# Eight gathers between the folds of the last gate, earlier routing steps on ScalarE, and rows spread evenly over the UP stage

## The reference, cut to what matters

```python
q = (h @ w_q).reshape(T, 8, 256)                       # T = 256 tokens, 8 heads
s1, s2 = q[..., :128] @ k1.T, q[..., 128:] @ k2.T      # 128 keys each
v1, i1 = top_k(s1, 16); v2, i2 = top_k(s2, 16)
top, pos = top_k(v1[..., None] + v2[..., None, :], 16) # 16 experts of 16384 a head
idx = take_along_axis(i1 * 128 + i2, pos)
act = gelu(einsum('thkd,td->thk', u_tab[idx], h)) * softmax(top)
ff = einsum('thk,thkd->td', act, v_tab[idx])
x = x + gt_f * rms_norm(ff, g_post_ffn)                # gt_f: the last gate, silu(c) @ w_ada + b_ada
```

## Time and profile before

| | us |
|---|---|
| median of 3 runs | 1793.8 |
| profiled execution | 1799.25 |
| its span | 1797.1 |
| TensorE busy | 1700.1 (95%) |
| VectorE busy | 1395.3 (78%) |
| ScalarE busy | 600.9 (33%) |
| GpSimd busy | 352.6 (20%) |
| moved by DMA | 646.75 MB, 360 GB/s |

### The profile page before, as it was taken

The page is one execution under the profiler, slowest core; times in us unless marked ns, Lnnn a source line. Parts: engine busy times, 40 slices in busy tenths (PEclk is TensorE's granted clock), DMA queues, the critical chain, the costliest instruction groups (busy, mean ns, idle before and its releaser), DMA issues.

```text
span 1797.1 us, 26702 instructions
## 1 busy us (share of the span) xinstructions
PE 1700.1 (95%) x9810; PEld 1475.6 (82%) x9810; DVE 1395.3 (78%) x2170; ACT 600.9 (33%) x1062; POOL 352.6 (20%) x266
## 2 busy tenths in 40 slices
PE   7999999999999899949999879999999999999998
PEld 6888888544999899949999879988778777777786
DVE  4668899967776497895876747169899998999997
ACT  3001222401543321013332103244444444544454
POOL 1000000011000121231122212014324333243310
PEclk9999999999999999979999999999999999999999
DMA  9998766799899999988999999799999999999995
GB/s 380 421 421 335 279 250 247 261 404 389 300 348 283 304 416 370 417 331 336 421 383 385 421 420 414 269 335 406 390 387 377 387 389 391 391 377 385 389 382 205
DMA packets 112121, 646.75 MB, mean 360 GB/s; under 512 B 16339, under 2 KB 16931, under 8 KB 50211
## 3 DMA queue, kind: packets, MB, share of 16 engines
q1 hardware_dynamic: 71570, 384.88, 55.2%
q0 software_dynamic: 34976, 252.75, 35.6%
q10 hardware_dynamic: 5488, 7.93, 1.6%
HBM read 639.08 MB, written 5.26 MB: 359 GB/s over the span
## 4 chain that ended last, share of the span: by engine, by line
PE 53%; DMA 25%; DVE 9%; issue 9%; ACT 2%; POOL 1%; DVEq 0%; ACTq 0%; SPq 0%; POOLq 0%
PE ps L1441 20%; PE ps L1082 14%; DMA raw<-in_peer_v 8%; DMA raw<-in_w_ada 7%; PE ps L1166 6%; PE ps L1336 4%; DMA third<-third 3%; DMA big<-in_u_rows,mid_info 3%; DVE raw L1500 2%; PE ps L1177 2%; DMA big<-in_u_rows,row_info 2%; PE ps L1282 2%; PE ps L1123 1%; DVE big L1860 1%; DVE w_low L1482 1%
## 5 line engine op out<-in xcount | busy, mean ns | idle before, releaser
L1082 PE MATMUL ps<-early,raw 128*128 128x144 f32 x3840 | 494.6, 290 | 25.4 <-DMA raw<-in_peer_u 24.7
L1082 PEld LDWEIGHTS ps<-early,raw 128*128 128x128 f32 x3840 | 485.1, 194 | 29.6 <-issue 14.8
L782 ACT ACTIVATE w_hi<-raw 128x1024 fp32r<-128x1024 f32 x204 | 214.7, 1060 | 290.9 <-PE ps L1441 180.5
L1482 DVE TENSOR_TENSOR w_low<-raw,w_hi 128x1024 fp32r<-128x1024 f32 x204 | 248.7, 1222 | 59.5 <-ACT w_hi L782 59.1
L1441 PE MATMUL ps<-w_low,a 128*128 128x512 f32 x1024 | 276.0, 391 | 14.1 <-DVE w_low L1482 14.1
L1441 PE MATMUL ps<-w_hi,a 128*128 128x512 f32 x1056 | 270.1, 391 | 2.4 <-ACT w_hi L782 1.7
L1441 PEld LDWEIGHTS ps<-w_low,a 128*128 128x128 f32 x1024 | 191.5, 188 | 58.9 <-DVE w_low L1482 19.4
L1441 PEld LDWEIGHTS ps<-w_hi,a 128*128 128x128 f32 x1056 | 198.6, 189 | 45.9 <-ACT w_hi L782 3.4
L1500 DVE CUSTOM_DVE_ANT_0 raw<-raw,big 128x2048 f32<-128x2048 f32 x64 | 146.0, 2291 | 56.7 <-DMA raw<-in_w_ada 56.7
L895 ACT ACTIVATE big<-ps 128x144 f32<-128x144 f32 x96 | 26.8, 291 | 284.7 <-PE ps L1082 266.1
L1441 PE MATMUL ps<-a 128*128 128x512 f32 x480 | 121.8, 389 | 0.0
(11 more groups left out here) (256 smaller groups left out, 2107.0 us busy)
## 6 DMA issues: line engine op xcount, KB each, us to landing
raw<-in_peer_u SPq DMA_DIRECT2D x128, 1024.0 KB, 10.8
raw<-in_peer_v SPq DMA_DIRECT2D x256, 512.0 KB, 9.9
early<-in_w_front SPq DMA_DIRECT2D x56, 1024.0 KB, 9.3
raw<-in_w_ada POOLq DMA_DIRECT2D x48, 1024.0 KB, 8.9
raw<-in_w_ada SPq DMA_DIRECT2D x32, 1024.0 KB, 12.6
raw<-in_peer_wq SPq DMA_DIRECT2D x16, 1024.0 KB, 6.6
big<-in_w_gate_f POOLq DMA_DIRECT2D x16, 1024.0 KB, 6.8
big<-in_x SPq DMA_DIRECT2D x2, 1024.0 KB, 6.3
```

Of the source, the lines that this page charges most:

```text
L782: act.activation(high_at(ph, j), raw[:, s % RING, :], ACT.Copy).then_inc(hi_ready, 1)
L1082: done = pe.matmul(ps[:, b % 4, 0:TU], raw[:, s % RING, k * P:(k + 1) * P], h[:, kc, 0:TU], start=kc == 0, stop=kc == KC - 1)
L1482: dve.tensor_tensor(w_low[:, s % RING, :], raw[:, s % RING, :], high_at(ph, j).bitcast(F32), ALU.subtract).then_inc(lo_ready, 1)
```

## The change

GpSimd: the folds become steps `fold(n)`; fold 0 and 1 come first, then row 0, then a row and a fold (or a small copy) in turn; the first eight rows use only two buffers (`TWO_BUFS`, `ROW_AT`), since the third still holds `acc_last`. ScalarE: `EXP_AT`, `PACK_AT` and `MID_PACK_AT` are 2 to 4 blocks (at the end more) earlier, `spread_h_rows` one block later, two waits are added. TensorE turns the picks behind block 30 instead of 34. VectorE: rows start one route later, one grid in six takes none, and no catching-up call follows the grids, so the tail takes 29 rows instead of 20. The order of kinds is 14 end, 32 four, 3 end, 16 eight, 19 end (before 12, 32, 10, 16, 14), and the copies, the mid gelu and the mid grids move to blocks 82, 104 and 110 (before 78, 103 and 108).

```diff
@@ -105,7 +105,7 @@
 EXTRA = TU - P
 MIDS = (("four", EXTRA + 16, 32, 32, 0), ("eight", EXTRA, 16, 16, 32))
 MID_ROWS = 48
-S_FIRST, S_BETWEEN = 12, 10
+S_FIRST, S_BETWEEN = 14, 3
 END_ROWS = [("end", n) for n in range(EARLY_ROWS)]
 ROW_ORDER = END_ROWS[:S_FIRST] + [("four", n) for n in range(32)] + END_ROWS[S_FIRST:S_FIRST + S_BETWEEN]
 ROW_ORDER += [("eight", n) for n in range(16)] + END_ROWS[S_FIRST + S_BETWEEN:]
@@ -113,15 +113,17 @@
 U_ROWS = len(ROW_ORDER)
 ROW_BUFS = 3
 THIRD = 2
+TWO_BUFS = 8
+ROW_AT = [n % 2 if n < TWO_BUFS else (n - TWO_BUFS + THIRD) % ROW_BUFS for n in range(U_ROWS)]
 QUADS, MID_QUADS, THIRDS = TU // 4, TM // 4, TU // TM
 GRID_AT = 56
 WINDOW, RING_UP = 40, 8
-EIGHTS_AT, MID_GELU_AT, MID_GRID_AT = 78, 103, 108
-TURN_AT = (GRID_AT - 3, 34)
+EIGHTS_AT, MID_GELU_AT, MID_GRID_AT = 82, 104, 110
+TURN_AT = (GRID_AT - 3, 30)
 H_UP_FROM = 8
-EXP_AT = (4, 6, 8, 11, 14, 18, 21, 25)
-PACK_AT = (7, 9, 12, 15, 18, 22, 25, 29)
-MID_PACK_AT = (30, 31)
+EXP_AT = (2, 4, 6, 8, 11, 14, 18, 21)
+PACK_AT = (4, 6, 8, 11, 14, 18, 21, 25)
+MID_PACK_AT = (26, 27)
 assert GRID_AT % 4 == 0 and GRID_AT + QUADS < MID_GRID_AT and MID_GRID_AT + MID_QUADS < EXPERT_BLOCKS - 4
 V_PER = ROWS // PH_DOWN.n
 V_FIRST, V_NEXT = ((0, 1, 4, 0), (1, 2, 0, 1), (2, 0, 1, 2)), (0, 1, 2, 3)
@@ -524,26 +526,34 @@
                     gp.wait_ge(ada_used, 2 * (g - 1))
                 gp.dma_start(gate_in_ring[:, g % 2, :], w_gate_f[g]).then_inc(gate_f_in[g % 2], 16)
 
-            gp.wait_ge(ada_used, 2 * KC)
-            for n, span in enumerate(FOLDS):
+            def fold(n):
+
                 if n:
                     gp.wait_ge(gate_f_sum, 16 * n)
+                span = FOLDS[n]
                 gp.dma_start(acc_last[0:span, :], acc_last[span:2 * span, :], accum_op=ALU.add).then_inc(gate_f_sum, 16)
+
+            def save_gate():
+
+                gp.wait_ge(gate_f_sum, 16 * len(FOLDS))
+                gp.dma_start(gate_saved, acc_last[0:1, :]).then_inc(gate_f_saved, 16)
+
+            def spread_gate():
+
+                gp.wait_ge(gate_f_saved, 16)
+                gp.dma_start(gate_cols, gate_saved[0, :].rearrange("(p a) -> p a", p=P)).then_inc(gate_f_saved, 16)
 
             def gather(n, table, where, done):
                 gp.indirect_dma_start(where, None, table, bass.IndirectOffsetOnAxis(ap=row_ix[:, n:n + 1], axis=0))\
                     .then_inc(done, 16)
 
-            gp.wait_ge(gate_f_sum, 16 * len(FOLDS))
-            gp.dma_start(gate_saved, acc_last[0:1, :]).then_inc(gate_f_saved, 16)
-            gp.wait_ge(gate_f_saved, 16)
-            gp.dma_start(gate_cols, gate_saved[0, :].rearrange("(p a) -> p a", p=P)).then_inc(gate_f_saved, 16)
-            gp.wait_ge(split_used, PH_UP.s)
-            for n in range(U_ROWS):
+            def u_row(n):
+
                 kind, row = ROW_ORDER[n]
-                if n >= ROW_BUFS:
-                    gp.wait_ge(row_used, n - ROW_BUFS + 1)
-                where, done = u_got[n % ROW_BUFS], row_in[n % ROW_BUFS]
+                buf = ROW_AT[n]
+                where, done = u_got[buf], row_in[buf]
+                if buf in ROW_AT[:n]:
+                    gp.wait_ge(row_used, max(r for r in range(n) if ROW_AT[r] == buf) + 1)
                 if kind == "end":
                     gp.wait_ge(*head_packed(row_info_in, row // HEAD_ROWS))
                     if n == 1:
@@ -556,9 +566,25 @@
                     gp.indirect_dma_start(where, None, u_rows,
                                           bass.IndirectOffsetOnAxis(ap=mid_ix[:, first + row:first + row + 1], axis=0)).then_inc(done, 16)
 
+            gp.wait_ge(ada_used, 2 * KC)
+            fold(0)
+            gp.wait_ge(split_used, PH_UP.s)
+            fold(1)
+            u_row(0)
+            for n in range(1, TWO_BUFS):
+                u_row(n)
+                if n + 1 < len(FOLDS):
+                    fold(n + 1)
+                elif n + 1 == len(FOLDS):
+                    save_gate()
+                else:
+                    spread_gate()
+            for n in range(TWO_BUFS, U_ROWS):
+                u_row(n)
+
             def last_use(buf):
 
-                return max(r for r in range(U_ROWS) if r % ROW_BUFS == buf) + 1
+                return max(r for r in range(U_ROWS) if ROW_AT[r] == buf) + 1
 
             def late_row(m):
 
@@ -940,6 +966,8 @@
             def scale_hots(q):
 
                 act.wait_ge(hot_made, q + 1)
+                if q == QUADS:
+                    act.wait_ge(picks_put, 3)
                 for t in range(4):
                     if q < QUADS:
                         scale = turned_picks[:, 4 * q // P, 2, 4 * q % P + t:4 * q % P + t + 1]
@@ -967,6 +995,7 @@
             for n in range(EXPERT_BLOCKS):
                 if n == EXPERT_BLOCKS - 2:
                     act.wait_ge(grid_used, QUADS)
+                    act.wait_ge(grid_put, QUADS + MID_QUADS)
                     high_group(0, None)
                     hi(PH_DOWN, 0, None)
                 if n == EXPERT_BLOCKS - 1:
@@ -981,7 +1010,7 @@
                         copy_scores(k)
                 if n == 2:
                     put_h_rows()
-                if n == 4:
+                if n == 5:
                     spread_h_rows()
                 if n in EXP_AT:
                     head_exp(EXP_AT.index(n))
@@ -1850,8 +1879,8 @@
                         dve.wait_ge(h_spread, 16 * 6)
                     if (kind, n) == ("eight", 0):
                         dve.wait_ge(h_spread, 16 * 14)
-                    dve.wait_ge(row_in[m % ROW_BUFS], 16 * (m // ROW_BUFS + 1))
-                    row, h, dot = u_got[m % ROW_BUFS], h_mid, None
+                    dve.wait_ge(row_in[ROW_AT[m]], 16 * ROW_AT[:m + 1].count(ROW_AT[m]))
+                    row, h, dot = u_got[ROW_AT[m]], h_mid, None
                     if kind == "end":
                         h, dot = h_tok, dots[:, n:n + 1]
                     else:
@@ -1920,7 +1949,7 @@
                 route(2 * b + 1)
                 if b:
                     finish_head(b - 1)
-                take_rows(2 if b > 2 else 0)
+                take_rows(2 if b > 3 else 0)
             for b in range(PEER_HEADS):
                 route(2 * b)
                 if b == 0:
@@ -1937,9 +1966,8 @@
                     hots(q + 2)
                 if q:
                     gate_made_acts(q - 1)
-                take_rows(1)
+                take_rows(q % 6 != 5)
             gate_made_acts(QUADS - 1)
-            take_rows(ROWS - rows_done[0])
             ring = 0
             for n in range(GRID_AT + QUADS + 2, EXPERT_BLOCKS + 1):
                 while GRID_AT + 4 * ring + 4 <= n and not (n < MID_GELU_AT and ring >= 11):
```

## The result

| | before | after |
|---|---|---|
| median | 1793.36 us (4 runs) | 1766.54 us (1761.06 to 1769.99, 4 runs) |
| profiled execution, its span | 1799.25, 1797.1 us | 1769.99, 1767.8 us |
| UP, first product to first matmul of DOWN | 550.8 to 1179.1: 628.3 us | 549.9 to 1151.4: 601.6 us |

The ratio is 0.9848, 95% interval [0.9808, 0.9888]: 27 us faster, where 1773 (1757 to 1790) had been forecast. Of each kernel the profiled execution is the longest one, and their difference is near that of the medians. All but 2.6 us of the span's 29.3 lie in UP.

What follows compares the result with a forecast made beforehand. The prediction took UP to be bound nearly as much by DMA as by TensorE. Its terms, -24 - 2.6 + 6 - 3 + 3 = -20.6, took the profiled 1799.3 to 1778.7, or 1773 us at the median (range 1757 to 1790).

Steps and rivals of the forecast that it cites:

- +8.6 for +6: UP ahead of block 54: three more gathers must be issued there, put at +6 us (0 to 12).
- -25.0 for -24: TensorE's 24.8 us wait for VectorE's routing behind block 53 falls to 0 or a few us: -24 us.
- -2.1 for -2.6: Three blocks behind that wait: the 2.6 us lost there to a lower clock are saved.
- -5.6 for -3: Grids' stage, blocks 54 to 91: 30 rows taken instead of 36, put at -3 us (-8 to +3).
- -2.6 for +3: Tail, blocks 92 to 127: it receives the rows taken off earlier, put at +3 us (-4 to +8).
- the two first steps: Early UP: earlier first exponential removes VectorE's 12.8 us wait; folds between gathers let row 0's gather out 31 us earlier.
- the first part: On what bounds the kernel: UP nearly as much by DMA as by TensorE, room only at 784 to 824 and 1118 to 1177.
- DMA is the bound and the gain is given back: Rival for UP: total bytes are the same, saving at most the idle capacity used; no change, 1793 us, chance 0.11.
- Waits for rows between folds: VectorE's routing: three pairs of rows at 22 us against 13.1 make it wait 27 us.
- the "above" bound of 21.4: GpSimd's fold steps behind gathers: at most a landed gather plus a fold, 12.6 + 8.8 us; 11 was taken.
- the rival in which folds pace the rows: Rival on GpSimd's queue: folds complete only after gathers, deciding from a 14.5 us step; slower, 1803 us, chance 0.11.
- the stall of VectorE for its first row: VectorE's wait for its first row in early UP: 7 us taken instead of 21.2.

Runs made afterwards that it cites:

- kernel 1: The kernel before with GpSimd's folds between the first eight gathers alone (and ScalarE's two added waits): 1789.24 us, ratio 0.998.
- kernel 2: The kernel before with ScalarE's steps alone moved forward, turn of the picks at block 30: 1795.77 us, ratio 1.0024.
- kernel 4: The kernel before with the rows' distribution alone changed (with b > 3), folds and ScalarE's steps as before: 1764.51 us, ratio 0.9849.
- kernel 9: The changed kernel with ScalarE's steps put back and the turn of the picks at block 34: 1764.96 us, ratio 0.9847.
- kernel 5: The kernel before with rows started one route later (b > 3) and fourteen end rows first: 1785.87 us, ratio 0.9972.
- kernel 3: The changed kernel with the rows' distribution of before; folds between gathers, earlier steps and b > 3 stay: 1782.43 us, ratio 0.9941.
- kernel 6: kernel 3 with the mid gelu at block 104 and the mid grids at 110, as in the change: 1785.8 us, ratio 0.997.
- kernel 11: The changed kernel with the first four copies of h_mid issued at block 22 instead of block 5: 1768.56 us, ratio 0.9873.
- kernel 12: kernel 4 with the first four copies of h_mid issued at block 22: 1767.02 us, ratio 0.9884.
- kernel 10: The changed kernel without the eight copies of h_mid at block 82, so part of the products is another computation: 1756.88 us, ratio 0.981.

## Why the prediction was right, and where its reasons were not

Its number came out within its range, 6 us above the measured one. By place, most terms hold. From block 0 to the end of block 53: 233.0 us before, 241.6 after, +8.6 for +6. At the turn: 25.5 us from the end of block 53 to block 54 became 0.5, -25.0 for -24. The three blocks behind it: 14.4 became 12.3, -2.1 for -2.6. From first to last of the 36 grids: 179.9 (823.7 to 1003.6) became 174.3 (804.3 to 978.5), -5.6 for -3. From there to DOWN: 175.5 became 172.9, -2.6 for +3: this term had its sign wrong.

By cause it was wrong, in the part "The change, part by part". It credited the -24 to the two first steps, ScalarE's timing and the folds between the gathers. Kernels 1 and 2 show these worth nothing alone, kernels 4 and 9 that they are worth nothing beside the rest. What made routing early enough was b > 3 and the order with fourteen "end" rows, named only in passing or not at all: kernel 5 cut the stall by 16 us with them alone. That the number came out all the same is in part luck: the change holds both these edits and the spread.

The weak step is the one that took the stages for independent, although the first part had just said that UP is bound nearly as much by DMA. Kernels 3 and 5 take 16 to 25 us off the stall and gain 5.5 to 10, because the 74 rows ahead of `gate_mids` still need their transfers, and the second part of UP grows by 10. The -24 at the turn stays, by kernels 4 and 9, where rows move behind `gate_mids` and into the last blocks. In the sum this move stood as a cost, +3, its 20 us of transfers nearly cancelled by room at the end of UP. The rival "DMA is the bound and the gain is given back" describes kernels 3, 5 and 6, where the rows were not moved, and there it holds in part: only 5.5 to 10 us of time are gained. That transfers are what the second part waits for fits every kernel here (rows every 4.97 us, 420 GB/s from 980 to 1069), but TensorE needs about as long, so what the spread would bring to a stage with less work on TensorE stays open.

Two sizes were off without harm. Waits for rows between folds were put at 27 us, and came to 7 (1.1 for the second row, then 3.5, 0.4 and 1.9). Of the four steps from fold to fold behind gathers, put at 11 us, one took 26.5, beyond the "above" bound of 21.4, and three took 11.0, 6.7 and 7.2. By the rule on ring order (the Trainium skill, "DMA: Bandwidth & Descriptors", "Queues, rings and completion order") a fold does stand behind the gathers issued ahead of it. The long step agrees: that fold landed 26.2 us after its issue, behind two gathers, where it took 6.5 alone. Six copies of the tokens went out on ScalarE's queue between 579.0 and 582.6, shortly before it, and no run tells the two causes apart; in kernel 9 the same fold took 15.0. It did no harm, since VectorE stood for those copies until 607.1 and GpSimd's next gather waited for that row. So the rival in which folds pace the rows, which needed 14.5 for every step, is refuted for this kernel, while its price was met once. And the stall of VectorE for its first row was 7.5 where 7 was put, but it waited for the tokens' copies, not for the row.

Left open: how much of the 51 us of capacity that are still unused can be had. 24 of them lie before 700, where 353 GB/s move at a DMA share of 0.99. What holds the rate down there is not shown, and moving the copies (kernels 11, 12) did not help.

## What to carry to other kernels

Where a stage moves fixed bytes near its highest rate, compute bytes over rate for the whole stage beside the waits, and don't add up the waits that vanish as if they were independent: here 16 us of stall removed gave 5.5 alone. Look at the last stretch of such a stage: a low rate there (279 GB/s of 421) can mean that work was done too early, ahead of something that others wait for, and it may be spread later. Take a change apart from both sides, by adding a part to before and by taking it out of after: removing 16 us of stall from before gave 5.5 us, putting 22.5 us of stall into after cost 14. When steps of a queue in order are moved forward, move what they wait for first, or the queue stands in front of everything behind it (kernel 2).

## What the runs showed of the hardware

Eight copies of `h_mid`, each 128 KB from DRAM to 16 partitions, cost more than their bytes. With them, 1.05 MB in all, 343 GB/s go in their 50 us, 404 without them (kernel 10). That is 3.05 MB less moved in all, 7.2 us at 421 GB/s, where a gather of the same size takes 2.5. UP as a whole got 5.0 us shorter without them. Whether it is the few partitions, no run shows. It happens at a DMA share of 1.01, and 420 GB/s go at the same share, so the share alone doesn't tell that the engines move at full rate.

A 128 KB fold on GpSimd's queue landed 6.5 us after its issue alone, and 26.2 us after it behind two gathers of 1.05 MB, with the tokens' copies under way on ScalarE's queue.
